# Listing the first expert job's rows early, and the other jobs' lists inside that job

## The reference, cut to what matters

```
h      = x1 * (1 + scale2) + shift2                     # "H2" here
logits = h @ w_router + b_router                        # 1024 x 32
top_v, top_i = top_k(logits, 4);  top_w = softmax(top_v)
for each expert e, for its tokens in blocks of up to 128 rows:
    gate = min(h[tok] @ w_gate[e] + b_gate[e], 7)
    up   = clip(h[tok] @ w_up[e] + b_up[e], -7, 7)
    act  = (up + 1) * gate * sigmoid(1.702 * gate)
    y[tok] += top_w * (act @ w_down[e] + b_down[e])
x = LayerNorm(alpha * x1 + gate2 * y)
```

## Time and profile before

| | |
|---|---|
| median of 3 runs | 2375.02 us (2374.65 to 2375.45) |
| the profiled execution | 2374.8 us |
| its span | 2373.1 us |
| mean granted TensorE clock | 0.959 |
| TensorE matmuls busy | 2184.6 us, 92% of the span |
| DVE, ACT, POOL busy | 1006.6, 452.7 and 445.9 us |
| chain that ended last | PE 85%, DVE 7%, DMA 4%, issue 2%, ACT 1% |
| DMA | 510.48 MB, mean 215 GB/s |

### The profile page before, as it was taken

How to read it: one execution, slowest core, us unless ns; L and a number is a source line. 1 busy time by engine, 2 the same in 40 slices (tenths; PEclk the granted TensorE clock), 3 DMA queues, 4 the chain that set the end, 5 groups by cost and what they waited for, 6 DMA issues and landing times.

```text
span 2373.1 us, 32923 instructions
## 1 busy us (share of the span) xinstructions
PE 2184.6 (92%) x9893; PEld 1013.8 (43%) x9894; DVE 1006.6 (42%) x1548; ACT 452.7 (19%) x579; POOL 445.9 (19%) x418
## 2 busy tenths in 40 slices
PE   6889999779956999999999999999999999999992
PEld 2444444464543444443443344444444444444441
DVE  3675743556663143344424243423253333223234
ACT  2334443331110111111111111111111111101113
POOL 0010000001212123222222132312123222122110
PEclk9989999889968999999999999999999999999996
DMA  9221320012242576889479999747899558886634
GB/s 330 80 81 53 110 59 27 1 72 91 103 181 93 202 293 213 298 308 376 163 267 400 362 349 405 262 157 245 300 381 351 183 177 294 301 311 234 232 88 170
DMA packets 169077, 510.48 MB, mean 215 GB/s; under 512 B 16333, under 2 KB 51329, under 8 KB 167883
## 3 DMA queue, kind: packets, MB, share of 16 engines
q1 hardware_dynamic: 153914, 474.25, 53.4%
q0 software_dynamic: 15120, 35.67, 6.9%
HBM read 480.51 MB, written 31.46 MB: 216 GB/s over the span
## 4 chain that ended last, share of the span: by engine, by line
PE 85%; DVE 7%; DMA 4%; issue 2%; ACT 1%; SPq 1%; POOL 0%; another core or an unknown queue 0%; DVEq 0%; POOLq 0%; ACTq 0%
PE psall L585 27%; PE psall L613 14%; PE psall L589 10%; PE psall L756 10%; PE psall L594 5%; PE psall L617 5%; PE psall L744 3%; PE psall L867 2%; PE psall L861 2%; PE psall L622 2%; DMA arena<-in_w_down_dram 1%; PE psall L654 1%; PE psall L723 1%; DMA arena<-in_x_dram 1%; DVE arena L1352 1%
## 5 line engine op out<-in xcount | busy, mean ns | idle before, releaser
L585 PE MATMUL psall<-arena 128*128 128x512 f32 x1472 | 648.8, 599 | 20.9 <-DVE arena L1637 12.8
L585 PEld LDWEIGHTS psall<-arena 128*128 128x128 f32 x1472 | 279.9, 192 | 368.9 <-issue 355.9
L613 PE MATMUL psall<-arena 128*128 128x512 f32 x736 | 323.6, 598 | 5.6 <-DVE arena L1686 2.7
L589 PE MATMUL psall<-arena 128*64 128x512 f32 x1152 | 259.3, 602 | 9.5 <-DMA arena<-in_w_up_dram 4.4
L1637 DVE STREAM_TRANSPOSE arena<-arena 128x1024 f32<-128x1024 f32 x49 | 61.0, 1245 | 479.0 <-PE psall L585 307.4
L756 PE MATMUL psall<-arena 128*128 128x512 f32 (+1 forms) x608 | 246.5, 563 | 0.7 <-ACT arena L976 0.7
L613 PEld LDWEIGHTS psall<-arena 128*128 128x128 f32 x736 | 139.6, 191 | 184.2 <-issue 184.2
L1149 ACT COPY arena<-psall 128x512 f32<-128x512 f32 x49 | 28.7, 586 | 793.6 <-PE psall L654 793.6
L1686 DVE COPY arena<-psall 128x512 f32<-128x512 f32 x49 | 33.9, 691 | 321.7 <-PE psall L654 321.6
L756 PEld LDWEIGHTS psall<-arena 128*128 128x128 f32 x608 | 116.5, 192 | 120.6 <-issue 116.3
L1626 DVE TENSOR_TENSOR arena<-psall,arena 32x256 f32<-32x256 f32 (+2 forms) x123 | 79.9, 649 | 203.2 <-PE psall L613 154.3
(11 more groups left out here) (286 smaller groups left out, 2013.0 us busy)
## 6 DMA issues: line engine op xcount, KB each, us to landing
arena<-in_w_gate_dram SPq DMA_DIRECT2D x128, 1024.0 KB
arena<-in_w_up_dram SPq DMA_DIRECT2D x128, 1024.0 KB
arena<-in_w_down_dram SPq DMA_DIRECT2D x128, 1024.0 KB
arena<-in_w_ada_dram SPq DMA_DIRECT2D x16, 1024.0 KB, 5.3
arena<-in_w_ada_dram SPq DMA_DIRECT2D x4, 2048.0 KB, 14.3
arena<-in_w_in_dram SPq DMA_DIRECT2D x16, 512.0 KB, 4.1
arena<-in_x_dram SPq DMA_DIRECT2D x2, 2048.0 KB, 28.4
arena<-in_w_out_dram SPq DMA_DIRECT2D x1, 4096.0 KB, 13.8
```

Of the source, the lines that this page charges most:

```text
L585: mm = pe.matmul(ps[2 * g + s], xT[:, k, :], w[:, s * BANK:(s + 1) * BANK], start=(k == 0), stop=(k == KD - 1))
L589: mm = pe.matmul(ps[2 * g][HT * j:HT * j + HT, :], xT[:, k, HT:P], w[:, j * BANK:(j + 1) * BANK], start=(k == 0), stop=(k == KD - 1), skip ...
L613: mm = pe.matmul(ps[6 + s], aT[:, k, :], w[:, s * BANK:(s + 1) * BANK], start=(k == 0), stop=(k == KD - 1))
```

## The change

What it does, in the order of the program:

- The scratch tiles of the lists (`tmpO`, `Gx`, `rt` and others) move to columns 18432 to 24576, in the down weights' ring slots; new small tiles stand behind them. The bias rows (`brow`) move into partition 0 of `adarow`, and `gidx` into another tile.
- TensorE turns X1 instead of H2. ACT applies the modulation as it copies to `h2T`, with a scale and a bias for each partition, in eight instructions of 128x128; for the last tile DVE does half of them. The scales and biases (`mod2`) come from 16 transposes of 2x128 ahead of the first out-projection. The router's weights come in their natural order by one DMA instead of eight.
- `select` gets two operations for the tile before: the running rank for expert 0 is copied (`first_ranks`), and a 128x128 matrix is made that has a one where a token's rank for expert 0 equals the slot (`first_slots`). `logits` of a tile waits for the whole selection of the tile before.
- Behind the last selection TensorE multiplies these with the token numbers (`first_rows`), DVE multiplies with a mask, one more matmul spreads the result, and two DVE operations give `gidx` for job 0. POOL gathers its rows at once (still behind all stores of H2), and then spreads the first bias rows.
- DVE makes the job table, then turns job 0's rows, then makes positions and matrices for all jobs. The list matmuls (`job_lists`) stand in TensorE's loop, between the first and the second half of gate and up, under a test that is true in the first round. They use banks 4 to 6.
- The places of missing rows in short first jobs go from the front to the back, with three more operations on 128x256 (`over`), and the gather of a short job starts at its first column block.
- POOL opens the down slots after the scatter's rows are made (third count of `moe_clear`).

```diff
-        o = O_X1 + 8192 + 2048
+        o = 18432
         tmpO = reg(o, NT, TOPK, NE); o += 1024
...
-        QUARTER_AT = {1: P - QR, 3: HT - QR}
+        QUARTER_AT = {1: 0, 3: HT}
...
             def turn_rows(T):
-                pe.wait_ge(h2_ready, T + 1)
+                pe.wait_ge(x1_ready, T + 1)
...
+            def first_rows(T):
+                pe.wait_ge(list_in, T + 1)
+                pe.matmul(ps[0][:, 0:TOPK], first_is[:, T, :], id1[:, T, :], start=(T == 0), stop=(T == NT - 1),
+                          skip_group_check=True).then_inc(list_mm, 1)
...
+            for q in range(2 * KD):
+                mm = pe.transpose(ps[6][:, 2 * NE + 2 * q:2 * NE + 2 * q + 2],
+                                  adarow[0:2, 1 + q // KD, (q % KD) * P:(q % KD + 1) * P], ident[0:2, 0:2])
+            mm.then_inc(mod_turned, 1)
...
+            pe.wait_ge(y_gated, 2 * NT)
+            for T in range(NT - 2):
+                first_rows(T)
             ranks(NT - 1)
...
+            first_rows(NT - 2)
+            first_rows(NT - 1)
             pe.wait_ge(list_ready, 1)
+            pe.matmul(ps[0][:, TOPK:2 * TOPK], spread4, first4, start=True, stop=True,
+                      skip_group_check=True).then_inc(list_mm, 1)
...
                         by_kind(pe, t, lambda kind: gate_up(pe, kind, u, on_, 0, KD // 2))
+                        with pe.If(u < 1):
+                            job_lists()
...
-                    act.copy(h2T[:, 4 * b:4 * b + 4, :], ps[4 + b][:, :].rearrange("p (a b) -> p a b", b=P)).then_inc(h2T_ready, 1)
+                    for k in range(4 * b, 4 * b + 4):
+                        mm = act.activation(h2T[:, k, :], ps[4 + b][:, (k % 4) * P:(k % 4 + 1) * P], ACT.Identity,
+                                            bias=mod2[:, 0, k:k + 1], scale=mod2[:, 1, k:k + 1])
+                    mm.then_inc(h2T_ready, 1)
...
+            def first_ranks(T, done):
+                dve.wait_ge(rank_mm, done)
+                link(dve.tensor_copy(rank0[:, T:T + 1], ps[7][:, T * NE:T * NE + 1]))
+
+            def first_slots(T):
+                dve.tensor_scalar(first_is[:, T, :], slots, rank0[:, T:T + 1], Mx[:, T, 0:1], ALU.is_equal,
+                                  ALU.mult).then_inc(list_in, 1)
...
+                    link(dve.tensor_reduce(spread4[:, 0:QR], ident[:, :].rearrange("p (t i) -> p i t", t=4), AX_X, ALU.add))
+                    link(dve.tensor_copy(spread4[:, QR:P].rearrange("p (a i) -> p a i", a=3),
+                                         spread4[:, 0:QR].unsqueeze(1).to_broadcast([P, 3, QR])))
+                    link(dve.tensor_reduce(quarter_of, ident[:, :].rearrange("p (t i) -> p t i", t=4), AX_X, ALU.add))
+                    for a in range(4):
+                        link(dve.memset(chunk0[QR * a:QR * a + QR, :], float(a - 4)))
...
+            dve.wait_ge(list_mm, NT + 1)
+            link(dve.tensor_scalar(first_id, ps[0][:, TOPK:2 * TOPK], 4.0, chunk0, ALU.mult, ALU.add))
+            dve.tensor_scalar(gidx.bitcast(I32), first_id, 0.0, None, ALU.max).then_inc(moe_clear, 1)
...
+            dve.wait_ge(xg_ready, 64)
+            turn_rows_in()
...
+            link(dve.scalar_tensor_tensor(out=over, in0=over, scalar=float(P), in1=pad_of, op0=ALU.is_ge, op1=ALU.mult))
...
             pool.wait_ge(moe_clear, 1)
-            gather(slice(1, 2), 1, 4)
+            rows_in(4)
+            pool.nop().then_inc(gidx_ready, 1)
+            pool.wait_ge(d_bias, 32)
+            pool.partition_broadcast(ebias[:, 0:2].rearrange("p a n -> p (a n)"), brow[:, 0:2 * D]).then_inc(bias_spread, 16)
...
+            pool.wait_ge(moe_clear, 3)
+            for b in range(2):
+                pool.wait_ge(x_stored[b], 8 * NT)
+            pool.nop().then_inc(dn_used, DNP)
```

More of the change, by code:

```diff
@@ L914, in _ @@
                       skip_group_check=True).then_inc(rank_mm, 1)
[L916 to L922, removed]
-            pe.wait_ge(list_ready, 1)
@@ L1130, in _ @@
                     std(T + 1)
-                for b in range(2):
+                if T == 0:
+                    act.wait_ge(ada1_ready, 2)
+                for b in range(2 if T + 1 < NT else 1):
                     act.wait_ge(h2_turned, 2 * T + b + 1)
@@ L1497, in _ @@
             select(NT - 2)
+            dve.wait_ge(h2_turned, 2 * NT)
+            dve.wait_ge(logit_mm, NT - 1)
+            for k in range(4, KD):
+                mm = dve.tensor_scalar(h2T[:, k, :], ps[5][:, (k % 4) * P:(k % 4 + 1) * P], mod2[:, 1, k:k + 1],
+                                       mod2[:, 0, k:k + 1], ALU.mult, ALU.add)
+            mm.then_inc(h2T_ready, 1)
             select(NT - 1)
             dve.tensor_tensor(ev, mx8[:, :, 0:TOPK], mx8[:, :, 0:1].to_broadcast([P, NT, TOPK]), ALU.subtract).then_inc(top_exp_in, 1)
-            dve.wait_ge(h2_turned, 2 * NT)
@@ L1611, in _ @@
-            link(dve.tensor_tensor(tok_f[:, :, 1:1 + JOBS], ids, gone, ALU.add))
-            dve.nop().then_inc(moe_clear, 1)
             def weigh(u, kind, order_):
@@ new lines, in _ @@
+            link(dve.tensor_scalar(r(NN), r(NQ), 1.0, None, ALU.min))
+            cumulative(IO, NN)
+            link(dve.tensor_scalar(r(N3), r(PAD), 1.0, None, ALU.is_equal))
+            cumulative(I3, N3)
+            U = small[:, 16:32]
+            uf = U[:, 0:1]
+            link(dve.tensor_scalar(uf, tok1, -1.0, None, ALU.add))
+            link(dve.tensor_scalar(r(T0), r(IJ), uf, None, ALU.is_le))
+            link(dve.tensor_reduce(U[:, 1:2], r(T0), AX_X, ALU.add))
+            link(dve.tensor_scalar(r(T0), iot, U[:, 1:2], None, ALU.is_equal))
@@ new lines, in _ @@
+            dve.wait_ge(list_mm, NT + 2)
+            dve.tensor_copy(rows2[:, 0], ps[4][:, 0:2 * JOBS].rearrange("p (j a) -> p j a", a=2)).then_inc(list_ready, 1)
+            dve.wait_ge(half_mm, 1)
+            chunk_ids = ps[5][:, 0:8 * JOBS].rearrange("p (t j a) -> p t j a", t=4, a=2)[:, :, :, 0]
+            for a in range(4):
+                q = slice(QR * a, QR * a + QR)
+                mm = dve.tensor_scalar(tok_g[q, :, 1:1 + JOBS], chunk_ids[q], 4.0, float(a - 4), ALU.mult, ALU.add)
@@ new lines, in _ @@
+            ids, gone = rows2[:, :, :, 0], empty
+            link(dve.tensor_copy(row_w[:, :, 1:1 + JOBS], rows2[:, :, :, 1]))
+            link(dve.tensor_scalar(gone, ids, 0.0, float(NOTOKEN), ALU.is_equal, ALU.mult))
+            link(dve.tensor_scalar(ids, ids, -1.0, None, ALU.add))
+            for h in range(2):
+                q = slice(HT * h, HT * h + HT)
+                link(dve.tensor_scalar(ids[q, 1], ids[q, 1], 2.0, float(h), ALU.mult, ALU.add))
+            for h in range(4):
+                q = slice(QR * h, QR * h + QR)
+                link(dve.tensor_scalar(ids[q, 2:4], ids[q, 2:4], 4.0, float(h), ALU.mult, ALU.add))
@@ L1778, in gather, with rows_in @@
                 settle(pool)
-                for t in range(4 - kind, 4):
+                rows_in(kind)
+            def rows_in(kind):
+                for t in range(kind):
                     pool.indirect_dma_start(out=xg[:, CW * t:CW * (t + 1)], out_offset=None,
```

263 lines of the change are left out of this document (130 added, 133 removed).

## The result

The changed kernel takes 2980.06 us (median of four runs, 2950.76 to 2993.37), the kernel before in the same session 2375.23: a ratio of 1.2519, 95% interval 1.2481 to 1.2557. The forecast was 2363.2, in a range of 2357 to 2371. The prediction was wrong by 617 us, and in sign.

A forecast was written before the change was run, and what follows sets the result against it. TensorE was taken as the bound, with 85% of the chain and a 56.8 us gap ahead of the job loop; 25.4 - 2.6 - 10.2 - 1.0 = 11.6 us off 2374.8 gave 2363.2 us, range 2357 to 2371.

The forecast's parts named there:

- The loop: TensorE's job rounds: one more test per round and a jump over the list code, +1.0 us, bounds 0 and 6.
- R3: Rival, chance 0.08: slower, the jump over the list code is exposed in every round, 17.8 us, giving 2380.0.
- R4: Rival, chance 0.05: no net change, several terms at their upper bounds together, 12.6 us more, giving 2375.8.
- R1: Rival, chance 0.13: larger gain, first job starts at 706 and the jump is free, giving 2359 us.
- X1[7]: Path to the last tile of X1, ready at 677.8 before: three added terms make it 2.6 us later.
- (a): 16 transposes of a 2x128 piece on TensorE in front of the first out-projection: +0.45 us.
- (b): Four constants made by DVE ahead of tile 1's gating delay its second half: +1.03 us, bounds 0 and 2.0.
- (c): ACT writes h2T in eight instructions instead of two, exposed at tile 5 ahead of the logits: +1.1 us.
- X1[7] to the first job: Stretch to job 0's matmuls: start at 709.2 instead of 734.6, -25.4 us, the table being the later path.
- Job 0: First job's gate and up: first half 17.0 us, list matmuls and spreading between halves +10.2, second half 13.7.
- Job 1's rows: Gather for job 1: rows land at 749.7, 3 us ahead of need; down weights counted as covered.
- R2: Rival, chance 0.13: POOL's loading on changing from bias broadcast to gather makes job 1's rows 7.5 us later, giving 2370.7.

The follow-up runs named there:

- e3: The kernel before with a test in each round of TensorE's job loop and one empty instruction under it, taken in round 0 only: 2374.22 us.
- e5: The kernel before with 50 matmuls in TensorE's job loop under a test true for no round that is run: 2373.59 us.
- e13: The changed kernel with 35 never-run matmuls at the start of TensorE's program, moving its code: 612 us less than the changed kernel.
- e14: As e13, and POOL opens the down slots only when DVE has turned job 1's rows: 2363.21 us.
- e1: The changed kernel with the list code and job 0's first half of gate and up ahead of the job loop: 2366.51 us, ratio 0.9982.
- e8: As e1, with job 0's second half ahead of the loop too, and down weights waiting for job 1's rows: 2374.3 us, ratio 1.0006.
- e16: The kernel before, loop untouched, with 56 never-run matmuls at the start of TensorE's program: not slow, 6 us above the 2375 expected.
- e9: The changed kernel with 100 semaphore increments at the start of TensorE's program, moving its code back: 3155 us.
- e12: As e9, and POOL opens the down slots only when DVE has turned job 1's rows; no time given, 9.1 packets a round.

## Why the prediction was wrong, point by point

**The step that failed: "The loop".** It took +1.0, bounds 0 and 6, for one more test in each round and a jump over the list code. The measured term is +609 us in the 51 rounds. The test and the jump cost nothing that is seen: e3, e5 and the rounds of e13 and e14 (1604.4 and 1604.0) show it. What the step left out is that the code jumped over is still part of the loop: 50 matmuls, 200 instructions, take it from 5.84 to 6.63 pieces, and where this loop begins it touches eight. Then the queue fetches 425 - 26 = 399 more packets, 7.8 a round. 609.1 / 399 = 1.5 us a packet. The waits on "issue" are 488 us in all and the lower clock 145 (together 633, with some 13 of it ahead of job 0, and less idle elsewhere). That a packet costs so much because it comes through DMA engines busy with weights is likely from the waits of e1 and e8 (3.90 and 14.02), but no run tests it in the rounds.

The Trainium skill, Advanced Engine Details and Errata, ISA Cache, describes it in part: TensorE has 128 KB for instructions, in lines of 16 KB or 256 instructions, and it warns of "Only 2 cache lines!". The packets of 16.4 KB agree with its line, and 128 KB would be eight lines. In these runs, by my count, seven stay and a loop that touches eight is fetched again. Two lines alone are not what binds TensorE here: the loop of 5.84 pieces ran its 52 rounds with 26 packets in all. Had I set the loop's length beside that figure, a rival at 6.63 pieces would have been within reach, though not its price.

**R3** had the right sign and place, and the wrong mechanism: it priced an exposed jump at 0.34 us a round, from the earlier trace rows. The loss is 11.9 a round, and no row of the kernel before could have given it: there the queue's 26 packets were a line to be read, not a time. **R4** came from the bounds together and fell with them. **R1** didn't occur: with the loop free, e14's first job starts at 714.79, later than the forecast, not earlier.

**X1[7].** Forecast +2.6. In the changed kernel it is ready at 681.43 + 1.22 = 682.65, which is +4.8. 2.0 of it is there at X1[0]; (a) asked 0.45, and the rest lies within what single executions differ by (above, under e16), so (a) can't be read. From X1[0] to X1[1] it is 15.67 after and 14.78 before: 0.89 for (b), where 1.03 was forecast. From X1[6] to X1[7] it is 19.77 and 17.80: 1.97 for (c), where 1.1 was forecast. The rows of (c) for tile 5, timeline of the changed kernel:

```profile
659.23 2.89 ACT L1169 ACTIVATE arena<-psall,ada 128x128 f32<-128x128 f32 x8
...
662.17 3.63 PE L899 MATMUL psall<-arena 128*128 128x32 f32 x16 [6.05 <-ACT arena L1169]
```

Eight take 2.89 us, not the 2.17 of the earlier trace rows: I had chosen the nearest size, and this form is dearer (0.36 against 0.27 each). 2.89 - 1.06 = 1.83. TensorE stands 6.05 idle for them ahead of tile 5's logits, 4.21 in the kernel before: 1.84 more.

**X1[7] to the first job.** Forecast start 711.8, measured 714.28, of which 2.2 is X1[7]'s. Job 0's list was ready at 701.36 + 0.17 = 701.53 (699 was forecast), and its first gather was issued at 702.46, within the 1 us of the signs. The order held: the table is what job 0 waits for, and its last register loads show as 2.18 on "issue" (1.7 forecast).

**Job 0.** The first half took 15.4 instead of 17.0, since the granted clock was 0.75 on average from 714.28 to 720.00 and not 0.50 as in the earlier trace rows; the lists and spreading 8.9 between the halves (729.68 to 738.59) instead of 10.2. Both errors were to the good and made up for the late start, which is luck. e14's job 0 ends at 739.14 + 13.95 = 753.09; the forecast had 752.7.

**Job 1's rows.** Forecast 749.7, 3 us early. They land at 746.83 + 8.23 = 755.06, and job 1 could have begun at 758.89 had its code been there. It wasn't POOL's loading (R2): its gathers are issued from 742.77 on. It is the down weights, which the change lets out at the same time: SP issues the first at 744.75, between the gathers of 744.26 and 745.58, and they fill the DMA engines in front of the rows. e14 takes that away, and job 1 begins at 756.81 (forecast 756.4) instead of e13's 761.62; the median falls by 4.6 us. Of the 4.81 between these two profiles 1.53 stood at X1[7] already (683.40 and 681.87), so that the wait itself is worth about 3.3. I had called the down weights "covered" by asking only when they are needed, not what they are in the way of.

So the terms before the loop add up to what was forecast for e14, which needed both a shift of code and a wait that the change doesn't have; that its 2363.21 meets the forecast's 2363.2 is an agreement of a kernel that wasn't the one forecast. Against the kernel before on its own chip it gains 14.2 where 11.6 was forecast, so the equal figures are luck besides.

**What stays open.** That seven pieces stay and eight don't, and where the pieces' edges lie, is inferred from these placements, not seen: the trace doesn't say which piece a packet brings. The four placements of 6.63 that are free (five kernels) span 0.39 of a piece where 0.37 would be allowed, five instructions more; perhaps the loop's last ones aren't needed each round. And e9 and e12 fetch 9.1 packets a round where the changed kernel fetches 7.8; why it is more than eight wasn't tried. e1 fetched 33 packets, though its loop ends at 22.90 + 5.84 = 28.74 pieces; that isn't explained either.

## What to carry to other kernels

Code that is skipped in a loop isn't always free: count the instructions of the engine's whole loop body, four for a float32 matmul and two for a transpose, and see how many pieces of 256 it touches, not only how long it is. When TensorE idles on "issue" throughout a loop, look first at the packets of the instruction queue, and move the code by a block that never runs before looking for a cause in the change. And when a change frees a large transfer earlier, ask whose small transfer it now passes.

## What the runs showed of the hardware

- A TensorE loop that by my count touched eight pieces of 16.4 KB was fetched again throughout (425, 426 and 488 packets in all, 2980 to 3155 us); every one that touched seven or fewer was not (26 to 33 packets, 2363 to 2386 us).
- A refetched packet cost about 1.5 us of TensorE's time in the changed kernel (609.1 / 399). The entry into the loop's code cost 3.90 us in e1, with the DMA engines all but idle, and 14.02 in e8, behind 4 MB of weights.
- The idle time costs again through the clock: 1.00 before the wait of 862.82, 0.50 in its windows from 869 on, and 8.60 instead of 7.09 us for the 32 instructions behind it.
- A compare and a jump in each of TensorE's rounds aren't seen (e3; the rounds of e13 and e14).
- A scaled and biased ACTIVATE of 128x128 out of PSUM takes 0.36 us; the form of the earlier trace rows takes 0.27.
